# One kernel of five parts: side-by-side first columns, interleaved weight splits, sums by token tile, an earlier end of the ada work, low parts made on GpSimd

## What is computed

```python
def ffn_step(t, sh, sc, g, wi, wo):
    return t + 0.5 * g * swiglu(modulate(rms(t), sh, sc), wi, wo)
# first block: layer 0 (mixer A), then layer 1 (mixer B); x and xc are 256 tokens each
mod = silu(c) @ ada_w[i] + ada_b[i]                 # 9 vectors of 1024: sh, sc, g for three steps
x = ffn_step(x, sh1, sc1, g1, pre_wi, pre_wo)       # and xc with its own vectors
x = x + g2 * mixer(modulate(rms(x), sh2, sc2))      # qkv, attention, w_o
x = ffn_step(x, sh3, sc3, g3, post_wi, post_wo)
# then twice: rms -> w_in -> RWKV-7, NSA and windowed attention -> gated merge -> w_out -> PEER
y = sum_over_8_heads_and_16_experts(gate * act(h . u_e) * v_e)     # PEER, rows gathered per token
# last: rms of the sum, with a gain
```

## Time and profile before

| | us |
|---|---|
| median of 3 runs (4340.87, 4355.53, 4351.46) | 4351.46 |
| the profiled execution's own time | 4335.86 |
| its span, with a mean granted TensorE clock of 0.97 | 4334.1 |
| PE busy | 3874.6 (89%) |
| DVE busy | 2660.9 (61%) |
| ACT busy | 1679.5 (39%) |
| POOL busy | 629.2 (15%) |

### The profile page before, as it was taken

The page is one execution under the profiler, slowest core; times in us unless marked ns, Lnnn a source line. Parts: engine busy times, 40 slices in busy tenths (PEclk is TensorE's granted clock), DMA queues, the critical chain, the costliest instruction groups (busy, mean ns, idle before and its releaser), DMA issues.

```text
span 4334.1 us, 50495 instructions
## 1 busy us (share of the span) xinstructions
PE 3874.6 (89%) x17500; PEld 2726.7 (63%) x17500; DVE 2660.9 (61%) x5369; ACT 1679.5 (39%) x3700; POOL 629.2 (15%) x665
## 2 busy tenths in 40 slices
PE   6999998999999999998999888778789998887777
PEld 4787765788788766997777743222377777442222
DVE  6877555666555546556346666677463466676774
ACT  3222535323322345542225444444422254444443
POOL 1100000000000000000000144344200001444442
PEclk9999998999999999999999999999999999999999
DMA  5554111454343310542133599999721335999997
GB/s 219 199 180 160 69 39 59 136 175 165 116 144 134 114 49 30 205 169 95 37 110 122 232 420 420 420 420 420 309 78 39 108 126 230 420 420 420 420 420 297
DMA packets 135007, 904.28 MB, mean 209 GB/s; under 512 B 14855, under 2 KB 15879, under 8 KB 35168
## 3 DMA queue, kind: packets, MB, share of 16 engines
q0 software_dynamic: 95552, 620.97, 35.5%
q1 hardware_dynamic: 39200, 280.08, 18.1%
HBM read 899.90 MB, written 5.28 MB: 209 GB/s over the span
## 4 chain that ended last, share of the span: by engine, by line
PE 62%; DMA 20%; DVE 10%; ACT 6%; issue 2%; DVEq 0%; POOL 0%; ACTq 0%; POOLq 0%
PE ps L652 36%; PE ps L447 19%; DMA arena<-peer_uv,arena 15%; PE ps L2452 6%; DMA silu_cc<-peer_uv,arena 4%; DVE w_lo L617 1%; DVE arena L706 1%; DVE arena L2601 1%; DVE ada_t L706 1%; ACT arena L2512 1%; ACT L2508 1%; DVE arena L1119 1%; ACT w_hi L599 1%; ACT L2480 1%; DMA arena<-adastream 1%
## 5 line engine op out<-in xcount | busy, mean ns | idle before, releaser
L2452 PE MATMUL ps<-arena 128*128 128x512 f32 x1640 | 812.3, 623 | 187.5 <-ACT arena L2512 185.9
L617 DVE TENSOR_TENSOR w_lo<-wt,w_hi 128x1024 fp32r<-128x1024 f32 x388 | 475.4, 1225 | 393.2 <-ACT w_hi L599 370.9
L652 PE MATMUL ps<-h_hi,w_hi 128*128 128x512 f32 (+1 forms) x1744 | 655.1, 376 | 64.4 <-DVE h_lo L727 44.7
L2601 DVE CUSTOM_DVE_ANT_0 arena<-arena 128x1024 f32<-128x1024 f32 x410 | 502.2, 1225 | 326.1 <-DMA arena<-peer_uv,arena 325.2
L2452 PEld LDWEIGHTS ps<-arena 128*128 128x128 f32 x1640 | 292.4, 193 | 637.3 <-ACT arena L2512 411.4
L2575 POOL DMA_INDIRECT arena<-peer_uv,arena x410 | 437.3, 1066 | 1644.9 <-DVEq L2566 1052.7
L599 ACT ACTIVATE w_hi<-wt 128x1024 fp32r<-128x1024 f32 x388 | 406.6, 1058 | 662.5 <-PE ps L652 635.6
L652 PE MATMUL ps<-h_lo,w_hi 128*128 128x512 f32 (+1 forms) x1744 | 645.5, 370 | 0.0
L652 PE MATMUL ps<-h_hi,w_lo 128*128 128x512 f32 (+1 forms) x1744 | 644.9, 370 | 0.0
L447 PE MATMUL ps<-hT,wt 128*128 128x256 f32 x1632 | 421.5, 390 | 6.0 <-issue 3.0
L652 PEld LDWEIGHTS ps<-h_hi,w_hi 128*128 128x128 f32 x1744 | 336.2, 193 | 136.0 <-issue 46.3
(11 more groups left out here) (337 smaller groups left out, 5480.2 us busy)
## 6 DMA issues: line engine op xcount, KB each, us to landing
wt<-wstream SPq DMA_DIRECT2D x262, 1024.0 KB, 4.8
ada_t<-adastream POOLq DMA_DIRECT2D x133, 512.0 KB, 3.6
arena<-peer_uv,arena POOLq DMA_INDIRECT x410, 20.3
arena<-adastream POOLq DMA_DIRECT2D x11, 512.0 KB, 26.7
bias_by_query<-bias_by_distance POOLq DMA_DIRECT2D x1, 4096.0 KB, 17.1
arena<-bias_by_query POOLq DMA_DIRECT2D x1, 3072.0 KB, 13.1
xT<-tokens SPq DMA_DIRECT2D x1, 2048.0 KB, 15.3
cst<-consts SPq DMA_DIRECT2D x1, 1816.0 KB, 9.2
```

What stands on the lines that cost most here:

```text
L617: self.step(self.dve.tensor_tensor(lo, raw_group(g), hi.bitcast(F32), ALU.subtract))
L652: ins = self.pe.matmul(o, a, b, start=start and i == 0, stop=stop and i == 2)
L2452: ins = pe.matmul(bank, diag[n % DIAGS], row[:, at:at + 512], start=s == 0, stop=s == SLOTS - 1)
L2601: dve.tensor_tensor_reduce(u, u, ztok[:, t], 1.0, 0.0, ALU.mult, ALU.add, hbuf[:, t, s:s + 1]).then_inc(dot_ready.sem, 1)
```

## The change

Five parts, each in plain words, then the core of the diff.

1. **First columns side by side.** In `PLAN` and on PE the first two columns of a_qkv and b_qkv, and the first four of a_w_o and b_w_o, are taken side by side: each input chunk now gives 6 or 12 matmuls.
2. **Groups between chunks.** In a_out, b_out and merge one weight group is split ahead of the input and three between its chunks (after chunks 2, 4, 6 of a_out's loop, after 1, 3, 5 in b_out, after 3, 7, 11 in the merge).
3. **Sums by tile.** The squares and sums that follow PEER are made in PEER: ACT squares a tile's half as soon as DVE has added it (tile 0 at (1, 3), tile 1 at the end), PE sums it with 128 columns, and rstd is made before the stage ends. `pe_norm` and `act_squares` go from the next rwkv_in and the final norm.
4. **Low parts on GpSimd.** The `w_lo` of groups 0 to 7 of the first stage are made by POOL (`pool_low`), between its ada loads; DVE no longer makes them, and waits for all eight after its last chunk.
5. **Ada work ends four groups earlier.** `dve_ffn` deals it over 62 places; the last four get none.

```diff
-    def square(name, layer, cols, rows=D):
-        for c in cols:
+    def square(name, layer, cols, rows=D, abreast=1):
+        for k in range(rows // P):
+            for c in cols[:abreast]:
+                add(name, layer, k * P, c)
+        for c in cols[abreast:]:
...
+    square("a_w_qkv", 0, range(0, 2 * D, P), abreast=2)
...
+    square("a_w_o", 0, range(0, D, P), abreast=4)
...
+        def pool_low(pool, step, g):
+
+            pool.wait_ge(w_hi_ready.sem, w_hi_ready.due(pool))
+            hi, lo = split_ring.bufs[g % SPLITS]
+            step(pool.tensor_tensor(lo, raw_group(g), hi.bitcast(F32), ALU.subtract))
+            pool.sem_inc(split_ring.full, 1)
+            if g % 2:
+                pool.sem_inc(w_free, 1)
+            pool.sem_inc(low_done, 1)
...
+            if abreast:
+                pe.wait_ge(r.free, r.given_back(abreast))
+                banks = [r.claim() for _ in range(abreast)]
+                for k in range(DC):
+                    pe.wait_ge(h_ready.sem, h_ready.due(pe))
+                    for c, bank in zip(cols, banks):
+                        SW.mm(bank[:, 0:T], three(SW.next(name, 0, k * P, c), h_parts(k, 0, T)), k == 0, k == DC - 1,
+                              r.full if k == DC - 1 else None)
+            for c in cols[abreast:]:
...
             dve_ada(dve, step, ADA_FIRST[:4])
-            weights = SplitLo(dve, step, groups, ahead=1)
+            weights = SplitLo(dve, step, groups, DC, DC)
+            w_hi_ready.due(dve, DC)
+            split_done[0] += DC
...
                 dve_low(dve, k, T)
-                if k < DC - 1:
-                    weights.ahead()
+            dve.wait_ge(low_done, DC)
...
-            ada = spread(ada, 2 * HALF_GROUPS)
+            ada = spread(ada, 2 * HALF_GROUPS - 4) + 4 * [[]]
...
-            weights = SplitHi(act, merge_groups(l))
-            for whole, hi, _ in TO_SPLIT:
+            weights = SplitHi(act, merge_groups(l), ahead=1)
+            for n, (whole, hi, _) in enumerate(TO_SPLIT):
                 act.activation(hi, whole, ACT.Copy).then_inc(h_hi_ready.sem, 1)
+                if n in (3, 7, 11):
+                    weights.ahead()
...
+        def pe_peer_sums(pe, mm, t):
+
+            for half in range(2):
+                pe.wait_ge(part_ready.sem, part_ready.due(pe))
+                for k in range(4 * half, 4 * half + 4):
+                    mm(total[:, t * P:(t + 1) * P], ones, hT[:, k, t * P:(t + 1) * P], k == 0, k == DC - 1,
+                       total_ready.sem if k == DC - 1 else None)
+
+        def act_peer_squares(act, t):
+            for half in range(2):
+                seg = slice(4 * half, 4 * half + 4), slice(t * P, (t + 1) * P)
+                act.wait_ge(res_ready.sem, res_ready.due(act))
+                act.activation(hT[:, seg[0], seg[1]], xT[:, seg[0], seg[1]], ACT.Square).then_inc(part_ready.sem, 1)
...
+            load_ln_exp(act)
+            act_peer_squares(act, 1)
+            act.wait_ge(total_ready.sem, total_ready.due(act, QT))
+            act_rsqrt(act, step, rstd[:, 0:LAT], total, 1.0 / D, eps)
+            act.sem_inc(rstd_ready.sem, 1)
...
-            stages.append(lambda: pe_norm(pe, mm, LAT))
+            stages.append(lambda: None)
...
-                    pool_ada(pool, ADA_FIRST + ADA_PRE0)
+                    blocks = ADA_FIRST + ADA_PRE0
+                    pool_ada(pool, blocks[:ADA_HELD + 2])
+                    for g in range(DC - 2):
+                        pool_low(pool, step, g)
+                    pool_ada(pool, blocks[ADA_HELD + 2:ADA_HELD + 4])
+                    pool_low(pool, step, DC - 2)
+                    pool_ada(pool, blocks[ADA_HELD + 4:ADA_HELD + 6])
+                    pool_low(pool, step, DC - 1)
+                    pool_ada(pool, blocks[ADA_HELD + 6:])
```

More of the change, by code:

```diff
@@ L110, in weight_plan @@
     align()
-    square("b_w_qkv", 0, range(0, D + 256, P))
+    square("b_w_qkv", 0, range(0, D + 256, P), abreast=2)
     for k in range(DC):
@@ L114, in weight_plan @@
     align()
-    square("b_w_o", 0, range(0, D, P))
+    square("b_w_o", 0, range(0, D, P), abreast=4)
     ffn("post", 1)
@@ L1152, in act_a_out @@
             load_ln_exp(act)
-            weights = SplitHi(act, with_next(groups_of("a_w_o", 0, D), ffn_groups("post", 0)))
+            weights = SplitHi(act, with_next(groups_of("a_w_o", 0, D), ffn_groups("post", 0)), ahead=1)
             for h in range(A_HEADS + 2):
@@ L1178, in dve_a_out @@
         def dve_a_out(dve, step):
-            weights = SplitLo(dve, step, with_next(groups_of("a_w_o", 0, D), ffn_groups("post", 0)))
+            weights = SplitLo(dve, step, with_next(groups_of("a_w_o", 0, D), ffn_groups("post", 0)), ahead=1)
             step(dve.tensor_scalar(small[:, 1:2], v("a_subln"), 1.0 - LAM_INIT, None, ALU.mult))
@@ L1192, in dve_a_out @@
                                       ALU.subtract).then_inc(h_ready.sem, 1)
+                if h in (2, 4, 6):
+                    weights.ahead()
             for m in range(DC):
@@ L2308, in dve_merge @@
         def dve_merge(dve, step, l):
-            weights = SplitLo(dve, step, merge_groups(l))
-            for whole, hi, lo in TO_SPLIT:
+            weights = SplitLo(dve, step, merge_groups(l), ahead=1)
+            for n, (whole, hi, lo) in enumerate(TO_SPLIT):
                 dve.wait_ge(h_hi_ready.sem, h_hi_ready.due(dve))
@@ L2384, in model_kernel @@
         diag_ready = signal("diag_ready")
+        total_ready = signal("total_ready")
+        total = ps[:, 4, 0:LAT]
         y_stored, y_turned = signal("y_stored"), signal("y_turned")
@@ L2626, in b_out @@
                 SW = SplitWeights(pe, W)
-                pe_split_project(pe, SW, "b_w_o", range(0, D, P), LAT, D_, True)
+                pe_split_project(pe, SW, "b_w_o", range(0, D, P), LAT, D_, 4)
                 SW.close()
@@ L2668, in b_out @@
                 load_ln_exp(act)
-                weights = SplitHi(act, with_next(groups_of("b_w_o", 0, D), ffn_groups("post", 1)))
+                weights = SplitHi(act, with_next(groups_of("b_w_o", 0, D), ffn_groups("post", 1)), ahead=1)
                 for k in range(DC):
                     act.activation(h_hi[:, k, 0:LAT], oB[:, k, :], ACT.Copy).then_inc(h_hi_ready.sem, 1)
+                    if k in (1, 3, 5):
+                        weights.ahead()
                 for m in range(DC):
@@ L2701, in _ @@
                 ]
[L2702 removed]
+            stages.append(lambda: act_norm(act, LAT, gained(act, "lnf", 0)))
             for n, s in enumerate(stages):
@@ L2713, in b_out @@
                 dve_bias(dve, step)
-                weights = SplitLo(dve, step, with_next(groups_of("b_w_o", 0, D), ffn_groups("post", 1)))
+                weights = SplitLo(dve, step, with_next(groups_of("b_w_o", 0, D), ffn_groups("post", 1)), ahead=1)
                 for k in range(DC):
```

30 lines of the change are left out of this document (16 added, 14 removed).

## The result

The change measured 4319.71 us (median of 4 runs, 4315.97 to 4327.09) against 4353.49 for the kernel before in the same comparison (4 runs, 4340.87 to 4362.93): a ratio of 0.9926, 95% interval 0.9897 to 0.9955. That is 33.8 us less, where 16 were forecast; the time lies within the stated range. Run once more with five rounds, it gave 4322.03 against 4351.70 (23 runs of before, 4335.8 to 4365.47): 0.9935, interval 0.9913 to 0.9957, or 29.7 us.

The account below looks back on a forecast made before the run. PE was taken to lead the chain (62%), with gathers pacing PEER, so edits pay where PE idles at stage ends. Terms summed to -15.9 us: 4319.9 for the profiled execution, 4335.5 for the median, range 4312 to 4351.

Parts of the forecast that it names:

- rival A: First stage: POOL's subtraction runs freely beside DVE, -10 in place of +9.3, total -35, 4316 us; chance 0.12.
- Low parts on GpSimd: First stage: POOL's subtractions and DVE's two-input instructions exclude each other, so moving eight low parts costs +9.3 us.
- L: Length of one POOL subtraction of 128x1024 in the first stage, bounded by 1.22 and twice that, taken as 2.60 us.
- six against five: First stage: six POOL subtractions fall in DVE's awaited chain, against five of DVE's own: 6 x 2.60 - 5 x 1.41 = +8.6.
- My sign of being wrong: First stage: the forecast is wrong if, among other signs, POOL's subtraction lies outside 1.2 to 2.6 us.
- Ada work: First and post-FFN of layer 0: stalls up to +2, last column's residual -1.2; taken as +1 us, from -3 to +5.
- qkv: a_qkv and b_qkv: with the first columns side by side, column 2 begins earlier, -4.5 and -6.1 us.
- Column 2 some 2.8 us behind the last chunk: a_qkv: sign to look for, column 2 starting about 2.8 us after the last input chunk.
- a_out 0, b_out -2.4, merges -2 each: Output stages and merges: a_out's gapless matmuls gain nothing; earlier PE starts give -2.4 in b_out, -4 over two merges.
- rival B: qkv, b_out and merge: earlier PE starts are lost to later waits, giving 6 instead of 17; total -5, 4346; chance 0.20.
- Sums by tile: Ends of both PEER stages: 4.9 to 6.2 us from last additions to next product, gaining -3.7 and -5.5 us.
- The step from execution to median: Whole kernel: the profiled execution was 15.6 us under the median, so 4319.9 became a median forecast of 4335.5.

Follow-up runs that it names:

- low_on_dve: The changed kernel, with the low parts of the first stage's first eight groups made by DVE again and POOL only loading: 4310.41 us, ratio 0.9910 to before.
- only_low: The kernel before with one part alone, POOL making the low parts of groups 0 to 7 of the first stage: 4364.96 us, ratio 1.0035.
- pool_beside: The kernel before with 30 useless 128x1024 subtractions on POOL during the attention of layer 0: 4390.05 us, one run.

## Why the prediction was right, and where not

**Sign and range: right.** The time fell by more than 0.3%, and 4319.7 lies between 4312 and 4351. It lies nearer to rival A (4316) than to the forecast (4335.5), but not by A's mechanism: GpSimd and DVE do exclude each other, and the part costs time. A is refuted by `low_on_dve`, `only_low` and `pool_beside`.

**Low parts on GpSimd: mechanism right, size too large.** Forecast +9.3, measured +4.9 to +5.0 at the last `h_lo`; the last chunk's first matmul came at 93.60, not at 98. Two terms were mis-sized. One is L: I took 2.60; DVE was held up by 2.05 as a rule. With 2.05 the same sum is 6 x 2.05 - 5 x 1.41 + 0.7 = +6.0. The other is the count: not six against five, but all eight subtractions held DVE up, against all eight of its own that went, and 16.5 - 11.3 = +5.2 meets the measured time. My sign of being wrong, a subtraction outside 1.2 to 2.6 us, did appear, as six of the eight are recorded with 2.79 to 3.35 us; the two looked at above take 2.23 and 2.24 without the wait ahead of them. The estimate of 2.25 from the Trainium skill ("GPSIMD Engine Reference", section 3.1) was nearer than mine, and its sum of +7 too. The port rule of the Trainium skill ("SBUF — State Buffer", section "SBUF: two separate sides") agrees with what `pool_beside` shows for operations with two SBUF inputs (751 to 2470 ns) and for those that read PSUM (1217 to 1212 ns).

**Ada work: wrong in sign.** Forecast +1. In the first FFN the shape was right: the stalls rose by 2.0 to 2.5 us and the tail gave back 2.3 (forecast +2 and -1.2), together about zero. But the post-FFN of layer 0 is 2.8 us shorter with 62 places than with 66 where DVE makes the low parts, and 0.8 and 2.4 us shorter in the two pairs of the change; the medians give the part 4.4 us. The step that failed is the tail: I priced it at -1.2, for the residual alone. PE waits 1.3 to 1.7 us less ahead of the closing sum, and the sum itself then took as little as 1.96 us, where it had taken 3.4 to 3.75.

**qkv: right.** -4.5 and -6.1 forecast, -4.0 and -4.5 measured. "Column 2 some 2.8 us behind the last chunk" came out as 2.75. For b_qkv the forecast of column 2 itself was right: it begins at 1525.01, 18.61 us behind the stage's first `hT`, where it was 24.65, so 6.0 us earlier. The step that failed was to take this for the gain of the whole stage. One more head sum stands among the next columns (0.56 us), and toward the stage's end, from 1584 on, PE was granted 1.2 GHz for 10 us, where before it was 7 from 1592 on (0.8 us between them).

**a_out 0, b_out -2.4, merges -2 each: right.** Measured +0.5 and -0.1; -2.2; -1.6 and -1.7. The gap before the merge shrank by 4.3 us and three fifths of that was lost again; 1.8 us of it are three new waits for DVE's `o_lo` and `z_lo`. In b_out PE's first wait shrank from 7.2 to 2.9 us and the wait ahead of the closing sum grew from 1.5 to 3.4. That is what rival B would have had everywhere.

**Sums by tile: too small.** -3.7 and -5.5 forecast, -5.3 and -6.4 to -6.5 measured between the additions and the next `hT`, which are now 4.63 us apart, under my 4.9 to 6.2. The mis-sized term is PE's. I took the upper of its two prices, 2.7 us behind ACT's last square. The sums of 128 columns took 2.05 us for all 16 rows, both halves, where the earlier trace rows have 5.38; the first half ran beside ACT's second square, and only 1.3 us were left behind it.

**The step from execution to median: wrong.** The terms measured in the waypoints add up to about -22: +5.0, -0.3, -4.1, +0.2, -1.6, -4.5, -2.2, -1.6, -5.2, and in the last row -1.7 at the second merge and -6.4 behind the second PEER. The sum forecast -16, so 6 us come from the mis-sized terms: the low parts 4 too dear, the ada work and the sums by tile 2 to 3 too small a gain each, the qkv 2 too large a one. The medians moved by 30 to 34. The rest, some 8 to 12 us, is left for the clock, by subtraction: I added the 15.6 us between the profiled execution and the median to both sides, as if they were a constant. They are the low stretches that the profiled execution of before happened not to have, up to 11 us each, and the changed kernel meets fewer of them. That it does so is shown by the profiles, for the attention of layer 1 (11 us), and goes with the narrower spread of its times (11 us over ten runs, where before has 30 over 23); why it does so is open. That -15.6 between the two first profiles matches -15.9 so closely is luck: -22 from the work and +6.4 from a low stretch.

## What to carry to other kernels

Before moving an elementwise operation to GpSimd, ask what DVE does meanwhile. If it is the engine waited for and reads two SBUF operands, nearly the whole length of GpSimd's operation, here 2.05 us of 2.24, is added to it, against 1.41 us saved; leaving the operation where it was gave the best version, 4310.4. Where a stage starts with an input that arrives in chunks, give each chunk more columns and split the first weights between the chunks: 4 to 5 us per qkv and 1.7 per merge, once per stage. Look at the end of a stage too: work that DVE does just ahead of a closing sum is paid by PE, here by up to 3.5 us in one FFN. And compare a profile with the spread of the times before making it the base of a sum: take two profiles, and look at the granted clock where they part.

## What the hardware showed that was not expected

- The same program differed by 24.3 us between two profiled executions, nearly all of it in three places where PE does many short matmuls and was granted 1.2 GHz for 20 us and more; the matmuls of one 24 us stretch fell from 114 to 64.
- The closing sum of the post-FFN of layer 0, four matmuls, took 3.41 to 3.75 us behind 3.45 to 3.81 us of idle PE in the nine profiled executions with 66 ada places, and 1.96 us behind 2.12 in both of the best version.
- A `TENSOR_SCALAR` on DVE is shut out by GpSimd as well: with one tensor operand and a scalar in SBUF it went from 539 to 1129 ns on average, and one on 128x2 elements from 0.23 to 2.13 us.
- A subtraction of 128x1024 on GpSimd was shown as 2.34 to 3.35 us long beside DVE, and the thirty of `pool_beside`, one behind the other, took 78.19 us, 2.61 each; in the first stage DVE felt 1.9 to 2.2 us of each.
